# Exchanging the two engines that search the top-k threshold in a fused decoder step

## The reference

```python
sc = jnp.where(vis, index_scores(iqb, ik, iwb), -jnp.inf)   # relu(iq . ik) weighted over 4 heads
_, sel = lax.top_k(sc, topk)                                # topk = 256
ok = sel <= tpos[None, :, None]
return sparse_attend(qb, gather_rows(k, sel), gather_rows(v, sel), ok)
```

## Time and profile before

| what | value |
|---|---|
| runs of the kernel before, median (3 runs) | 4142.27 us (4137.85 to 4146.02) |
| profiled execution: span from first to last instruction | 4139.1 us |
| median less that span | 3.2 us |
| TensorE matmul busy, of the span | 84% |
| VectorE busy | 45% |
| ScalarE busy | 33% |
| GpSimd busy | 21% |
| mixer stage, tiles 1 to 15 of the attention | 614.1 to 1863.9 us |

### The profile page before, as it was taken

One profiled execution on the slowest core, in us unless ns is written; L12 is line 12 of the kernel. 1 busy time (PEld: TensorE's weight loads), 2 busy tenths in 40 slices (PEclk: granted clock), 3 DMA queues, 4 the chain that ended last, 5 costly groups with the idle time before them and its releaser, 6 DMA issues. The chain is left out here.

```text
span 4139.1 us, 47583 instructions
## 1 busy us (share of the span) xinstructions
PE 3468.1 (84%) x15449; PEld 2016.0 (49%) x15449; DVE 1876.7 (45%) x3884; ACT 1383.0 (33%) x2827; POOL 858.9 (21%) x1709
## 2 busy tenths in 40 slices
PE   7999648999999897786367999989989956997998
PEld 4445324555555555563223444444444534665665
DVE  0000046677777877333810240431511546774674
ACT  1111126656666565640111111111111123442442
POOL 3112253222211110000000000000000006774672
PEclk9999868999999997787688999999989977997999
DMA  7334324544433330003314012011021032223321
GB/s 244 105 96 129 101 76 153 160 141 143 121 112 112 102 94 14 3 3 120 138 47 186 33 44 66 25 56 51 27 65 41 23 112 75 93 93 92 113 82 57
DMA packets 233111, 366.74 MB, mean 89 GB/s; under 512 B 45876, under 2 KB 130909, under 8 KB 228733
## 3 DMA queue, kind: packets, MB, share of 16 engines
q1 hardware_dynamic: 208064, 334.62, 25.2%
q10 hardware_dynamic: 20736, 21.05, 1.5%
q0 software_dynamic: 4096, 8.40, 0.8%
HBM read 279.22 MB, written 106.04 MB: 93 GB/s over the span
## 5 line engine op out<-in xcount | busy, mean ns | idle before, releaser
L1930 PE MATMUL QB<-hT,w_c 128*128 128x512 f32 x1024 | 449.4, 593 | 0.0
L328 PE MATMUL P0A<-w_all,hT 128*128 128x512 f32 (+1 forms) x1200 | 431.7, 521 | 0.0
L631 PE MATMUL PB<-wb,hT_ahead 128*128 128x512 f32 x704 | 366.1, 646 | 3.2 <-ACT prb L751 1.9
L655 PEld LDWEIGHTS PO<-vst,ptT 128*128 128x128 f32 x2176 | 295.4, 207 | 81.5 <-issue 43.6
L655 PE MATMUL PO<-vst,ptT 128*128 128x64 f32 x2176 | 308.7, 287 | 13.4 <-ACT ptT L771 13.2
L328 PEld LDWEIGHTS P0A<-w_all,hT 128*128 128x128 f32 x1200 | 207.5, 191 | 219.6 <-issue 219.6
L1930 PEld LDWEIGHTS QB<-hT,w_c 128*128 128x128 f32 x1024 | 190.0, 190 | 217.1 <-issue 217.1
L1875 PE MATMUL QS<-w_o,yT 128*128 128x512 f32 x544 | 274.6, 669 | 17.4 <-ACT yT L2043 17.4
L642 PE MATMUL PT<-ident,sm 128*128 128x128 f32 x1088 | 198.8, 308 | 106.0 <-ACT sm L763 105.8
L1899 PE MATMUL QA<-w_c,hT 128*128 128x512 f32 (+1 forms) x768 | 254.8, 488 | 5.7 <-ACT hT L2059 5.7
L771 ACT COPY ptT<-PT 128x512 f32<-128x512 f32 (+3 forms) x320 | 164.9, 518 | 275.1 <-PE PT L642 274.1
(11 more groups left out here) (412 smaller groups left out, 5317.7 us busy)
## 6 DMA issues: line engine op xcount, KB each, us to landing
wb<-in_w_in_ab SPq DMA_DIRECT2D x176, 512.0 KB, 3.7
out_c_all<-crow SPq DMA_DIRECT2D x256, 64.0 KB, 1.6
w_all<-in_w_in_ab SPq DMA_DIRECT2D x48, 256.0 KB, 8.1
out_pr_all<-pr_out SPq DMA_DIRECT2D x17, 546.0 KB, 2.9
pra<-out_pr_all SPq DMA_DIRECT2D x16, 546.0 KB, 4.6
x_rows<-in_x_all SPq DMA_DIRECT2D x17, 512.0 KB, 5.5
yab<-out_yab_all SPq DMA_DIRECT2D x17, 512.0 KB, 3.6
xin<-in_x_all SPq DMA_DIRECT2D x17, 512.0 KB, 4.2
```

Of the source, the lines that this page charges most:

```text
L328: ins = pe.matmul(PA[u % 6][:, 0:b - a], hT[:, t % (LAG + 2), c, :], w_all[:, c, a:b], start=(c == 0), stop=(c == KD - 1))
L631: ins = pe.matmul(PB[:, :], hT[:, 2 * q + k, :], wb[:, u % 4, k, :], start=(q == 0 and k == 0), stop=(q == 3 and k == 1))
L655: ins = pe.matmul(PO[:, h * HD:(h + 1) * HD], ptT[:, v % 2, k * P:(k + 1) * P], vst[:, 4 * c + k, a * HD:(a + 1) * HD], start=(c == 0 and ...
L1930: ins = pe.matmul(PB[b % 2][:, 0:N], w_c[:, c, b * P:(b + 1) * P], hT[:, c, 0:N], start=(c == 0), stop=(c == KD - 1))
```

## The change

Even and odd tiles exchange their form of search. Odd tiles (3, 5, ..., 15) are now searched by counting on VectorE, even ones (2, 4, ..., 14) by sign sums on ScalarE. Places, steps, widths, waits and all other work stay.

```diff
+def by_sums(s):
+
+    return s % 2 == 1
+
+
 def search_step(add, place, s, k):
 
-    if s % 2 == 0:
+    if by_sums(s):
         add(place, "dve", "count", s, k)
     else:
         add(place, "act", "signs", s, k)
@@ bounds
-                if f % 2 == 0:
+                if by_sums(f):
                     link(dve.tensor_tensor(rng, hi, lo, ALU.subtract))
...
```

## The result

The kernel after took 4158.5 us (median of 4 runs) beside 4140.1 us for the kernel before on the same chip, a ratio of 1.0046 with a 95% interval of [1.0029, 1.0063]: slower, and outside the forecast range. Its profiled execution, the fastest of the four (4153.7 us), spans 4152.1 us against 4139.1 us, +13.0 us, at a mean granted clock of 0.891 against 0.893. The profiles can explain these 13.0 us; the rest of the 18.4 us between the medians is scatter between executions.

The account below looks back on a forecast made before the run. Up to block 12 TensorE bounds the mixer stage, in blocks 13 and 14 a chain; -1.8 (blocks 2 to 12), +2.2 (13) and +0.2 (14) give +0.6 us on 4142.27, so 4142.9 us; range 4132 to 4154.

Parts of the forecast that it names:

- the one on blocks 8 and 12: Mixer stage: with 5.0 us to a block, block 12 becomes 107.3 and block 8 87.3 us, -3.6 and -1.8.
- a B: Block where VectorE does steps 12 to 23 of tile n+1 and ScalarE steps 0 to 11 of tile n+2.
- the stretch that the prediction built on: Third to fourth exponentials: 33.0 us in block 12, 24.8 in block 11, taken to show how the kinds of block differ.
- Blocks 9, 10 and 11: Mixer stage: taking on their neighbours' kind of block, they change by +2.1, -2.4 and +3.0 us.
- The first rival: Blocks 2 to 12: the alternation of block times isn't the searches', so they give 0; 4144.7 us; 16%.
- Blocks 2 to 7: Mixer stage: blocks 7, 5, 3 lose 1.3, 0.8, 0.3 us and 6, 4, 2 gain 1.0, 0.5, 0; together +0.9.
- The carrying down: Below block 8 the difference between the kinds of block falls by about half a microsecond to a block; +0.9 us.
- Price of a count: VectorE search step at 2048 columns: 2.86 us, bounds 2.72 and 3.0, from rank's count of the same operation and width.
- Block 13: First quarter +2.2, third -1.3, fourth +2.9, behind rank -1.9, wider counts +0.3; sum +2.2 us, bounds -1 and +6.
- Block 14: Takes VectorE's half instead of ScalarE's: first quarter +3.6, third -1.0, fourth -2.7; sum +0.2 us, bounds -6 and +5.
- Second rival: Blocks 13 and 14: slower because TensorE's granted clock falls to 0.62 and 0.66; +8.5 us, 4151.4 us; 20%.
- Its second price: 4156 us: the clock falls in blocks 13 and 14 and the savings on ScalarE are missing as well.

Follow-up runs that it names:

- after_51: Kernel after with block 8's count at place 51 (step 20 of tile 9) moved behind the masked at 51.33; 1.0017 of the kernel before.
- late_before: Kernel before with the count at place 75 (step 10 of each counted tile) moved behind rank and mask, to 81.5; 4126.3 us, 0.9959 of before.
- the last pair of kernels: Both orders with the count at 75 behind rank and idle matmuls in TensorE's waits, order of after also with block 8's count moved; 0.9915 (before's order) and 0.9937.
- the shifted ones: Kernel before with five or ten idle matmuls ahead of the third transposes of block 7, order otherwise kept; 1.0001 and 1.0019 of before.
- late_15: Kernel after with the count at 75 moved behind rank for tile 15 alone, that is, in block 13 alone; 1.0017 of the kernel before.
- from_five: Kernel before with the search forms exchanged only for tiles 5 to 15, so blocks 0 to 2 stay as before; 1.0042 of before.
- late_after: Kernel after with the count at 75 of every counted tile moved behind rank and mask, to 81.5; 4129.8 us, 0.9963 of the kernel before.

## Why the prediction was wrong

The step that failed is the one on blocks 8 and 12: "Blocks 12 and 8 have a B on one side only; with 5.0 us to a block [...] they become 107.3 and 87.3: -3.6 and -1.8." They became 110.8 and 98.3 us, 3.5 and 11.0 us more than that. These 14.5 us are more than the whole error against the profiled span (13.0 measured, 0.6 forecast); against the median the error is 15.6 us (4158.5 and 4142.9). The step took the alternation of neighbours for a property of the kind. Between blocks 9, 10 and 11, with the same chunk counts, it is one. Blocks 8 and 12 have other neighbours: block 7's tile has one chunk less than 8, block 9's index tile one more than 8's, and 12 stands alike between 11 and a block without index tile. In block 8 this puts a weigh, the count and a masked on one spot; after_51 shows that this spot cost 6.1 us. The rest of both shows in the quarters. In block 12 the stretch that the prediction built on did shrink, from 33.0 us to 29.7:

```profile
1552.56:1582.22 29.66, 23.34 (x126) 14.04 (x125) 24.77 (x41) 15.96 (x31) 1.69 (x1) 0.93 0.19 54
```

But the first quarter grew from 15.9 to 17.8 us and the second from 24.3 to 25.6, and that took it back. In block 8 the same stretch had little to lose: 23.5 us before, 23.4 with the count at 75 moved away (late_before), 23.2 in after_51; the first quarter grew by 2.5 to 2.9 us. That is also why the fourth quarter shrinks so little in the last pair of kernels: the count whose place made the difference is moved behind rank in both (in late_before that alone took block 12's stretch from 33.0 to 30.4 us).

The other terms were off as well and nearly cancel: the arrival at tile 0 (+6.7, priced at nothing), block 1 (+2.1, nothing), blocks 2 to 7 (9.6 us less than forecast), blocks 9 to 11 (1.2 more), blocks 13 and 14 (7.6 less), block 15 (+4.5, nothing) and the stages behind (+0.7).

Point by point:
- Blocks 9, 10 and 11: forecast +2.1, -2.4, +3.0; measured +3.0, -2.5, +3.4. The first rival (the alternation isn't the searches') fell.
- Blocks 2 to 7: forecast +0.9; measured -8.7, of which block 4 is 5.4 (and block 1, priced at 0, +2.1). Before, block 4 took 75.1 us with 13.7 us at half clock; it took 69.4 to 71.5 us in every kernel with the new order and without idle matmuls, with 6.8 to 10.2 us at half clock, and 72.9 and 73.0 us in the shifted ones with the old order and 6.8. So some 2 us there are clock and the other 3 the order of work; I had priced the block at -0.5. The carrying down itself was uneven (0.5 us from block 8 to 7, then about 0.25 to a block); half a microsecond throughout gives +0.8 for +0.9.
- Price of a count: 2.86 forecast, 2.77 measured. The duration, 2343 ns at 2048 columns, confirms the row of rank that the forecast used. The Trainium skill's 1227 ns (*VectorE: DVE Perf Modes*, section "The perf-mode tier table (the rule you actually need)") doesn't hold for this form with a sum.
- Block 13: the wait of 13.6 us came as 14.1. The third exponential was forecast to start about 1.0 us behind its maxima and starts 0.95 behind (1646.63 and 1647.58). The copy that TensorE waited 2.25 us for now costs 0.27. But two terms didn't come. The first quarter, priced at +2.2, grew by 0.4 (15.1 to 15.5 us), and the stretch from the third to the fourth exponentials, which was to grow by 2.9 with the wait, shrank from 29.6 to 28.7 us. The block went from 101.5 to 97.9 us instead of +2.2, with 20.7 us less at half clock. late_15 shows the fourth quarter's part alone: the wait is 2.6 us shorter without the count.
- Block 14: first quarter forecast 15.8, measured 15.8; no wait before rank; the third quarter went from 20.1 to 14.6 us, forecast -1.0; the whole +0.2 forecast, -1.6 measured.
- Block 15: priced at nothing, +4.5 us, half clock 34.2 us for 20.5. Its order of work is untouched by the change.
- Second rival, slower by TensorE's clock: the sign came, the place didn't, so the nearness of its prices (4151.4 and 4156, measured 4158.5) is luck. Its second price is also missummed: the savings on ScalarE that it leaves out are 1.3, 1.9, 1.0 and 2.7, together 6.9 us, which gives 4158.3. It was to decide in blocks 13 and 14, whose clock rose. The clock bit in block 8, behind a 2.0 us wait in a block that TensorE fills, where half clock is paid nearly in full. The Trainium skill's rule on waits between bursts of matmuls (*TensorE: Matmul & The Clock Gate*, section "HAM oscillation — how this bites in real kernels") agrees with block 13 of the kernel after, where the clock falls inside the 14.11 us wait and TensorE works at half clock from the end of that wait, 1678.2 us, to the end of the block. Its example has waits of about 3 to 5 us; the 2.01 us of block 8 are shorter, and were followed by half clock in the kernel after and by full clock in from_five and late_after.

The final account of the 12.3 us in blocks 8 to 15: 6.1 by block 8's meeting of three steps (shown by its removal), 3.1 by the rest of block 8, 3.9 in blocks 9 to 11 (the alternation as forecast), -0.1 in block 12, and -0.7 in blocks 13 to 15, where shorter and longer half-clock stretches nearly cancel. This is the account of this kernel's two profiles and not a fixed price of the order: from_five divides nearly the same sum otherwise, and blocks 1 to 7 gave 6.7 us back. What remains open is why blocks 14 and 15, with the same order of work, take 179.8 us in the kernel after and 197.6 in late_15, why the clock falls behind block 8's wait in some kernels and not in others, and whether the late arrival at tile 0 belongs to the change. The last one matters: in the first pair of profiles it is more (6.7 us) than all that the kernel after loses between tile 0 and tile 15 (5.6), in the second 6.2 against 9.2. With the two counts moved the orders stand at 0.9960 and 0.9959; with TensorE kept busy as well, some 12 us between them come back, so the two places aren't all of the exchange's price.

## What to carry to other kernels

When two halves of a schedule are exchanged, don't interpolate from neighbouring blocks: lay the new places beside the old ones where loop counts change, and look for a long step that now stands between an awaited one and the one that the busiest engine waits for. A 2 us wait in a block that TensorE fills cost three times its length where the clock fell behind it, and about its length where it didn't; a wait that grew to 14 us by a count, in a block with slack, showed nothing in the block's time. And a step that nobody waits for yet belongs behind the one that ends the quarter: moving one count behind rank gained 0.4% in the order of before and 0.7 to 0.8% in that of after, though in the order of before more than half of it came by the clock, in blocks where nothing had moved. Where a change is worth less than 0.5%, take a second profile of both kernels and add up by stage: two shifts that cancel (here +6.7 ahead of tile 0, -6.7 in blocks 1 to 7) hide behind one equal start.

## What the runs showed that I had not expected

- The same 2.01 us wait at the same place was followed by 10.2 us at half clock in the kernel after, by full clock in from_five and late_after.
- The blocks of one program repeat to 0.1 us between two profiles (blocks 1 to 15 of before, 8 to 15 of after), while arrivals at tile 0 differ by up to 8 us and the untouched stages behind by up to 10 us from profile to profile.
- Runs of one program spread by 0.5% with their mean clock (4132.9 us at 0.895, 4154.5 us at 0.889), and one arrangement (late_15) has three runs near 4139 us and nine from 4148 to 4166 us.
- Idle matmuls that fill TensorE's waits bring 0.6%, and 0.9% together with the late count, though they add work: the mean clock goes from 0.893 to 0.917.
- Five idle matmuls of 512 columns cost 3.9 us in a block that TensorE bounds.
